# Expert matmuls in plain fp32 in four column quarters, and weight rows of 4 KB, in a two-layer decoder step

## What is computed

```python
logits = (t @ w_router).astype(jnp.float32)
top_logits, top_idx = lax.top_k(logits, TOP_K_EXPERTS)          # 2 of 8
gates = jax.nn.softmax(top_logits, axis=-1)
combine = jnp.sum(jax.nn.one_hot(top_idx, N_EXPERTS) * gates[..., None], axis=1)
for e in range(N_EXPERTS):
    out = out + combine[:, e:e + 1] * swiglu(t, w_gate[e], w_up[e], w_down[e])
# swiglu(h, g, u, d) = (silu(h @ g) * (h @ u)) @ d;  g, u: 1024 x 3584,  d: 3584 x 1024, all fp32
```

## Time and profile before

| | |
|---|---|
| time, median of 3 runs | 1491.48 us (1490.03 to 1492.24) |
| span of the profiled execution | 1489.5 us |
| experts, first matmul to the one before the last scatter | 532.7 to 1481.9 us of the span |
| weight tiles of the experts | 168 of 2 MB |

### The profile page before, as it was taken

The page is one execution under the profiler, slowest core; times in us unless marked ns, Lnnn a source line. Parts: engine busy times, 40 slices in busy tenths (PEclk is TensorE's granted clock), DMA queues, the critical chain, the costliest instruction groups (busy, mean ns, idle before and its releaser), DMA issues.

```text
span 1489.5 us, 21413 instructions
## 1 busy us (share of the span) xinstructions
PE 1476.5 (99%) x8116; PEld 1258.8 (85%) x8116; DVE 1196.2 (80%) x1088; ACT 975.1 (65%) x933; POOL 162.4 (11%) x159
## 2 busy tenths in 40 slices
PE   8999999999999999999999999999999999999998
PEld 6987699999988978888888888888888888888887
DVE  5698576665556688888888888888889888888987
ACT  5444464443455587777777777777777778777775
POOL 3653000000000048200001001001000000000100
PEclk9999999999999999999999999999999999999999
DMA  7562983427554379999999999999999999999990
GB/s 256 194 260 71 391 307 114 170 100 253 186 186 155 111 258 390 362 395 383 394 393 382 396 393 382 394 395 382 393 394 360 394 393 370 386 390 362 371 366 32
DMA packets 196822, 456.64 MB, mean 307 GB/s; under 512 B 9988, under 2 KB 13102, under 8 KB 196762
## 3 DMA queue, kind: packets, MB, share of 16 engines
q1 hardware_dynamic: 188912, 439.60, 79.6%
q0 software_dynamic: 4336, 13.15, 3.1%
q10 hardware_dynamic: 3514, 3.08, 0.7%
HBM read 443.78 MB, written 12.03 MB: 306 GB/s over the span
## 4 chain that ended last, share of the span: by engine, by line
PE 94%; DVE 2%; ACT 1%; SPq 1%; issue 1%; DMA 1%; DVEq 0%; ACTq 0%
PE bank L2041 25%; PE bank L2570 13%; PE bank L2572 13%; PE bank L2571 13%; PE bank L2584 7%; PE bank L2586 7%; PE bank L2585 7%; PE bank L2594 2%; PE bank L2246 1%; DMA ring<-in_attn_w_in 1%; PE bank L2258 1%; PE bank L2220 1%; PE bank L2339 0%; DVE wql L1827 0%; SPq L686 0%
## 5 line engine op out<-in xcount | busy, mean ns | idle before, releaser
L1827 DVE TENSOR_TENSOR wql<-ring,wqh 128x2048 fp32r<-128x2048 f32 x335 | 766.8, 2291 | 107.3 <-ACT wqh L994 106.5
L994 ACT ACTIVATE wqh<-ring 128x2048 fp32r<-128x2048 f32 x334 | 641.5, 1921 | 230.8 <-PE bank L2572 148.4
L2570 PE MATMUL bank<-wqh,xgh 128*128 128x512 f32 x892 | 353.7, 396 | 0.2 <-DVE wql L1827 0.2
L2571 PE MATMUL bank<-wql,xgh 128*128 128x512 f32 x896 | 349.2, 390 | 0.0
L2572 PE MATMUL bank<-wqh,xgl 128*128 128x512 f32 x892 | 348.0, 390 | 0.0
L2572 PEld LDWEIGHTS bank<-wqh,xgl 128*128 128x128 f32 x892 | 167.5, 188 | 35.9
L2570 PEld LDWEIGHTS bank<-wqh,xgh 128*128 128x128 f32 x892 | 167.5, 188 | 34.4 <-DVE wql L1827 1.0
L2571 PEld LDWEIGHTS bank<-wql,xgh 128*128 128x128 f32 x896 | 168.5, 188 | 32.9
L994 ACT ACTIVATE wd<-ring 128x1024 fp32r<-128x1024 f32 x90 | 95.1, 1059 | 133.4 <-PE bank L2041 133.4
L2584 PE MATMUL bank<-wqh,heTh 128*128 128x512 f32 x440 | 171.4, 389 | 0.0
L2586 PE MATMUL bank<-wqh,heTl 128*128 128x512 f32 x440 | 171.2, 389 | 0.0
(11 more groups left out here) (457 smaller groups left out, 1962.6 us busy)
## 6 DMA issues: line engine op xcount, KB each, us to landing
ring<-in_moe_w_gate SPq DMA_DIRECT2D x56, 2048.0 KB, 15.2
ring<-in_moe_w_up SPq DMA_DIRECT2D x56, 2048.0 KB, 15.1
ring<-in_moe_w_down SPq DMA_DIRECT2D x56, 2048.0 KB, 15.2
ring<-in_attn_w_in SPq DMA_DIRECT2D x6, 2048.0 KB, 15.8
ring<-in_ffn_w_gate SPq DMA_DIRECT2D x5, 2048.0 KB, 16.3
ring<-in_ffn_w_up SPq DMA_DIRECT2D x5, 2048.0 KB, 10.9
ring<-in_cache_k SPq DMA_DIRECT2D x16, 512.0 KB, 6.5
ring<-in_cache_v SPq DMA_DIRECT2D x16, 512.0 KB, 5.7
```

Source lines behind the costliest of these rows:

```text
L994: return nc.scalar.activation(dst, src, ACT.Copy)
L1827: return v.tensor_tensor(dst, src, head.bitcast(F32), ALU.subtract)
L2570: mm(bank, xgh[:, k, :], w_h[:, part], start=(k == 0), stop=False)
L2571: mm(bank, xgh[:, k, :], w_l[:, part], start=False, stop=False)
```

## The change

The items have 96 slots, as three groups of 32. Matmuls are plain fp32 on unsplit weights, read straight from the ring, and each uses one quarter of the array's columns: 32 slots stationary (128 x 32), 256 (or 128) weight columns streaming, the result in 32 partitions of a PSUM bank. A "round" of four such matmuls fills the four quarters. Quarters 0 to 2 hold the three slot groups on the same quarter of the chunk's weight columns; quarter 3 takes the one slot group that is left over for the fourth quarter of the columns, so that three rounds cover 3 groups x 4 column parts. Chunks are 1024, 1024, 1024 and 512 columns wide; the wide gate and up chunks come as two tiles of 512 rows x 4 KB (`h` is the half), the last one as a tile of 1024 rows x 2 KB as before. There are still 21 tiles of 2 MB per item. `head`, `tail`, `wqh`, `wql`, `q_head` and `q_tail` are gone; a ring buffer is free when PE has used the tile (`q_used`). Indirect DMAs move 96 rows instead of 128.

```diff
-NCH = DFE // CH
+WIDE = [1024, 1024, 1024, 512]
+FROM = [0, 1024, 2048, 3072]
+NCH = len(WIDE)
+ROUNDS = 3
...
+GRP = 32
+SL = 3 * GRP
+MAXBLK = (T + SL - 1) // SL
...
         def expert_tile(e, g, kind, c, h):
...
-                src = w[bass.ds(e, 1), :, CH * c:CH * c + CH].rearrange("o (k p) f -> p (o k) f", p=P)
-                sp.dma_start(tile_cols(s, CH), src).then_inc(got, 16)
+                k = SLOT // wide
+                src = w[bass.ds(e, 1), P * k * h:P * k * h + P * k, FROM[c]:FROM[c] + wide]
+                sp.dma_start(ring[s][:].rearrange("p (k f) -> p k f", k=k),
+                             src.rearrange("o (k p) f -> p (o k) f", p=P)).then_inc(got, 16)
...
-                sp.wait_ge(q_tail, i * HI + (U0 + 2 * (g - RING + 1)))
+                sp.wait_ge(q_used, i * PER_ITEM + (U0 + g - RING + 1))
...
-            pool.indirect_dma_start(out=z_rows, out_offset=bass.IndirectOffsetOnAxis(ap=slots_to[:, 0:1], axis=0),
-                                    in_=ysb[:], in_offset=None, compute_op=ALU.add).then_inc(z_in, 16)
+            pool.indirect_dma_start(out=z_rows, out_offset=bass.IndirectOffsetOnAxis(ap=slots_to[0:SL, 0:1], axis=0),
+                                    in_=ysb[0:SL, :], in_offset=None, compute_op=ALU.add).then_inc(z_in, 16)
...
         def silu(i, c):
-            nc.scalar.activation(he[:], banks[c % NCH % 2][:], ACT.Silu).then_inc(sg_ok, 1)
+            n = WIDE[c % NCH] // 4
+            act.wait_ge(*after(i, UP, c))
+            for r in range(ROUNDS):
+                nc.scalar.activation(he[:, r, 0:n], pair_banks(c)[r][:, 0:n], ACT.Silu).then_inc(sg_ok, 1)
...
-        def tail(i, n):
-
-            dve.wait_ge(q_head, i * HI + (n + 1))
-            minus(lo_buf(n), half_of(n // 2, n % 2), hi_buf(n)).then_inc(q_tail, 1)
...
-        def half_tile(i, n, kind, c, last_item=False):
...
+        def of_round(r, q):
+
+            return (q, r) if q < ROUNDS else (r, ROUNDS)
+
+        def gate_or_up(i, g, kind, c, h):
+
+            wide = WIDE[c % NCH]
+            n, ks = wide // 4, SLOT // wide
+            pe.wait_ge(*arrival(i, g))
+            w = ring[expert_slot(g)][:].rearrange("p (k f) -> p k f", k=ks)
+            for j in range(ks):
+                k = ks * h + j
+                for r in range(ROUNDS):
+                    out = pair_banks(c)[r][:, n * kind:n * kind + n]
+                    for q in range(4):
+                        tokens, cols_ = of_round(r, q)
+                        last = mm(out[GRP * q:GRP * q + GRP, :], xg[:, k, GRP * tokens:GRP * tokens + GRP],
+                                  w[:, j, n * cols_:n * cols_ + n], start=(kind == GATE and k == 0), stop=(k == KD - 1),
+                                  skip_group_check=True)
+            last.then_inc(q_used, 1)
+
+        def down(i, g, c, h, src, by_round=False):
...
+            for r, j in steps:
...
+                for q in range(4):
+                    tokens, cols_ = of_round(r, q)
+                    left = src[:, per * part + b, GRP * tokens:GRP * tokens + GRP] if part < ROUNDS else \
+                        src[:, per * tokens + b, SL:P]
+                    last = mm(sums_of(r)[GRP * q:GRP * q + GRP, :], left, w[:, j, 256 * cols_:256 * cols_ + 256],
+                              start=first, stop=(c == NCH - 1 and j == CH // P - 1), skip_group_check=True)
```

More of the change, by code:

```diff
@@ L621, in token_rows, with last_tile, after, pair_banks @@
         return htok[NS * low:NS * low + NS, 4, :]
[L623 to L642, removed]
+    def last_tile(kind, c):
+        return NPRO + max(n for n, tile in enumerate(BODY_TILES) if tile[:2] == (kind, c))
+    def after(i, kind, c):
+        return q_used, i * PER_ITEM + (U0 + last_tile(kind, c) + 1)
+    def pair_banks(c):
+        return banks[ROUNDS * (c % 2):ROUNDS * (c % 2) + ROUNDS]
+    def sums_of(r):
+        return banks[6 + r // 2][:, 256 * (r % 2):256 * (r % 2) + 256]
+    BASE = {q_used: U0, y_out: 2}
     def start_counters(engine, *sems):
@@ new lines, in scatter_samples @@
+            part, left = slice(CH * half, CH * half + CH), pickT[0:SL, NP + NS * (1 - half):NP + NS * (1 - half) + 2 * NS]
+            mm(bank[0:2 * NS, :], left, ysbh[0:SL, part], start=(half == 0), stop=False)
+            return mm(bank[0:2 * NS, :], left, ysbl[0:SL, part], start=False, stop=(half == 1))
+        def of_round(r, q):
[7 more added lines that the diff above has]
+                k = ks * h + j
+                for r in range(ROUNDS):
+                    out = pair_banks(c)[r][:, n * kind:n * kind + n]
[5 more added lines that the diff above has]
+            last.then_inc(q_used, 1)
@@ new lines, in down @@
+        def down(i, g, c, h, src, by_round=False):
+            per = WIDE[c] // 4 // P
+            pe.wait_ge(*arrival(i, g))
+            w = ring[expert_slot(g)][:].rearrange("p (k f) -> p k f", k=CH // P)
+            steps = [(r, j) for r in range(ROUNDS) for j in range(CH // P)] if by_round else \
+                [(r, j) for j in range(CH // P) for r in range(ROUNDS)]
+            for r, j in steps:
+                part, b = (CH // P * h + j) // per, (CH // P * h + j) % per
+                first = c == 0 and h == 0 and j == 0 and r != 1
+                for q in range(4):
[4 more added lines that the diff above has]
+                              start=first, stop=(c == NCH - 1 and j == CH // P - 1), skip_group_check=True)
+                if by_round and r == 1 and j == CH // P - 1:
+                    last.then_inc(y_half, 1)
@@ L2589, in half_tile @@
             last.then_inc(q_used, 1)
         def turn(i, c):
-            pe.wait_ge(he_ok, i * NCH + (c + 1))
-            for j in range(4):
-                last = tr(banks[6][:, P * j:P * j + P], he[:, P * j:P * j + P], ident[:])
+            per = WIDE[c] // 4 // P
+            for part in range(ROUNDS):
+                pe.wait_ge(he_ok, i * PARTS + (ROUNDS * c + part + 1))
+                for b in range(per):
+                    at, most = per * part + b, 2 * per
+                    last = tr(pair_banks(c)[at // most][:, P * (at % most):P * (at % most) + P], he[:, part, P * b:P * b + P], ident[:])
```

447 lines of the change are left out of this document (197 added, 250 removed).

## The result

| | before | with the change |
|---|---|---|
| time, median of 4 runs each | 1491.06 us (1490.03 to 1492.24) | 1559.22 us (1555.54 to 1562.45) |
| ratio | | 1.0457, 95% interval 1.0443 to 1.0471 |
| span of the profiled execution | 1489.5 us | 1553.4 us |
| first expert matmul to the last one | 532.7 to 1481.9: 949 us | 532.3 to 1545.9: 1014 us |

The kernel became 68 us slower; 79 us less had been forecast. The trunk and the tail are as long as before (532 us, and 7.5 against 7.6 us), so all of it lies in the experts. The page of the changed kernel: busy time, the slices of the granted clock and of GB/s, the queues, the chain, and the groups of matmuls of gate and up (L2550) and of down (L2569).

A forecast was written before the change was run, and what follows sets the result against it. PE bounds the kernel, DMA a close second; afterwards DMA: 535 + 822 (tiles) + 19 (POOL's transfers) + 22 (boundaries) = 1398, plus 1 + 2.6 + 8.5 = 1410, plus 2 = 1412 us; range 1392 to 1450.

The forecast's parts named there:

- PE, matmuls: Expert matmuls on PE: 0.216 us per round of four, 2.6 us per tile instead of 5.45, 57.6 us per item.
- upper bound of 113.0 us per item: PE's expert work if each of 1104 matmuls per item cost 0.0995 us, plus 3.2 us; the lower bound was taken instead.
- starts of rounds of four 0.216 us apart at length: Sign in PE's expert timeline that the forecast holds; 0.43 would say the clock rival, uneven starts the PE-feeding rival.
- 402 matmuls at 0.0995: Earlier trace's 40 us of mixed and larger PE shapes, 0.0995 us each, used as evidence against PE being unfed.
- Rival C: Expert stage: PE cannot be fed, slower than today above 0.1046 us per matmul; 1522 us at 0.108; chance 0.06.
- DVE, ACT: cost 0: Experts: subtractions and copies go, small steps come; nothing gained directly, transposes' waits for `he` stay covered, cost 0.
- Ring: cost 0: Weight ring: buffers held until PE has used them, yet six tiles still queued at the DMA engines, cost 0.
- DMA: Expert weight loads: 5.07 us per 4 KB-row tile, 5.43 per 2 KB-row tile, 107.2 us per item plus 3.2 for scatter and gather.
- Rival A: Gate and up loads: strided 4 KB rows no better than 2 KB rows, 32 us more, 1444 us; chance 0.12.
- A boundary: Between expert items: scatter and gather disturb the weight stream by 3.2 us, seven times, 22 us.
- Rival B, the clock: Expert stage: half-busy PE drops to half clock, 115.3 us per item; 1466 us if held through; chance 0.06.
- Tail: After the last expert matmul: 7.6 us today plus about 0.9 for moving 32 x 256 pieces, 8.5 us.

The follow-up runs named there:

- e6: e2 with the narrow chunk's inner gate and up blocks as half as many 256-column matmuls, same column count: 1449.38 us, ratio 0.9725.
- e1: The changed kernel with expert matmuls reading the upper halves of the fp32 operands as bf16, one record per matmul: 1437.81 us, ratio 0.9647.
- e7: The kernel before, with PE's loop holding two items per turn and the last two items written out: 1499.4 us, ratio 1.0063.
- e2: The changed kernel with PE's loop over the items written out eight times, so no jump: 1493.6 us, ratio 1.0008.
- e5: The changed kernel with its jump, but after the first 25 expert tiles each load brings only 64 columns: 1484.82 us in one run.
- e3: The changed kernel with rounds 1 and 2 left out except for each sum's first and last block, all DMAs kept: 1438.72 us, ratio 0.9657.
- e4: e3 with the wide gate and up chunks loaded as 2 KB rows instead of 4 KB: 1464.27 us, ratio 0.9826.
- e8: e3 with the accumulating scatter after each of the first seven items replaced by a plain 4 KB store: 1428.07 us, ratio 0.9576.

## Why the prediction was wrong

Two steps failed. The first puts PE level with DMA and is worth 11 us of the result; the second is worth 110.

**The first is "PE, matmuls"**: "16 of them take 1.07 us". The rows are right, the noun is not. The earlier trace rows say x16, and the program's loop over the heads makes 8 matmuls of that shape per batch: each plain fp32 matmul leaves two records. I took records for matmuls, and so read 0.216 us per round where it is 0.432. Both numbers lay open, the records in the trace and the loop in the code, and I divided only one by the other's unit. The 512-column rows that seemed to confirm it share the mistake (x32 for 16 matmuls). The fp32r matmuls before leave one record each, so nothing in their rows gives a warning. With 112.0 in place of 57.6 us per item PE would have come out level with DMA (my 110.4), and the sum at 532.7 + 896 + 8.5 + 2 = 1439 us or more, a gain of 3.5% at best. e6 is this case, with PE fed: 1449.4 us, still inside my 1392 to 1450. e1 shows the step from the other side: one record per matmul, and the forecast picture appears. The Trainium skill says the same in its own way: its page "FP8 and Floating Point Precision", section "TensorE Precision Notes", has true fp32 take four passes through the array. Estimated from that page, a round of 256 columns is 1024 cycles, 0.43 us at 2.4 GHz, and the trace agrees with 0.432 us. I had not weighed that rule, and it spoke against this change. That my upper bound of 113.0 us per item comes so near to the 112.0 is luck: it was worked out from 402 records of other shapes, which I took for matmuls as well. And one sign that I had set, "starts of rounds of four 0.216 us apart at length", is there to the letter, since it was made with the same mistake.

**The second is that the sum has nothing for feeding PE**, on the ground of "402 matmuls at 0.0995". Rival C had it as "PE cannot be fed" from 0.1046 us per matmul on, chance 0.06, and its outcome came about: (1014/8 - 3.2)/1104 = 0.112 us, of which 252 x 0.432/1104 = 0.099 are the fp32 work itself. Its reasons were not the right ones. All four quarters overlap and issuing is no limit by itself (e1); the code of an item no longer stays with the engine and is fetched anew, 16 KB at a time, at every turn (e7), slowly after a jump (e2 minus 66 us) and too slowly for 128-column matmuls (e6 minus 44 us more), all the slower as weights fill the DMA engines (e5). The 402 of the earlier trace rows were no argument: those 40 us took three instruction packets, one per 13 us, and an item of the changed kernel takes 19 in 130 us, one per 7 us. The Trainium skill, page "Runtime: NRT & Kernel Launch", section "Instruction fetch mechanics", tells of blocks of 16 KiB, 128 KiB for PE, and says that a jump to a place outside the current two pages stops the engine until the page has come. The runs agree on the packet and on the stop. They don't agree on the two pages: the kernel before jumps back over 79 KB, five packets, and fetches nothing, so the border lies between 79 and 158 KB. Nor do they agree that fetching is otherwise mostly hidden, as the section has it: e2 has no jump and stands 30 us.

**DVE, ACT: cost 0** was right: DVE is at 27%, ACT at 21% of the span, and PE has no wait for the three parts of `he`.

**Ring: cost 0** was right where it can be seen, in e3 and e1, where a tile lands 24.3 us after its start, so the queue stays deep. In the changed kernel PE gives the buffers back late, and only some two tiles are queued (10.0 us to landing).

**DMA: right in kind, 24 us too low.** The last tile's matmuls would start at 1399 and start at 1422.5 us in e3. Tiles of 4 KB rows take 5.13 and not 5.07 us, 9 us in all; the instruction packets, not in the sum, are 3 us there (1.16 MB); some 12 us are not traced to a cause. The saving by 4 KB rows was put at 89 x 0.36 = 32 us and is 25.6 us (e4 against e3), 0.29 us per tile. Rival A is refuted. The rule of the Trainium skill that was weighed in the prediction (page "DMA: Bandwidth & Descriptors", section "Why small descriptors are slow (HBM only)") had 2.2% for it; the runs do not agree, they say 5.3% (0.29 of 5.42). A boundary was put at 3.2 us; its scatter costs 1.5 (e8), its gather was not tried.

**Rival B, the clock**, happened: the granted clock falls when PE waits, to 0.82 over the span in e1 and 0.90 in e3. It cost nothing there, since DMA sets the pace in both, and the two differ by 1 us. In the changed kernel, where PE is on the path, it cost 23 us after the waits. **Tail**: 7.5 us instead of 8.5.

In short, of the 147 us between forecast and result, 27 are DMA's floor (e3), 11 are PE's work in fp32 that lies above it (e6), and 110 are instructions that come late (44 in the narrow chunk, 66 by the jump), with the half clock behind these waits in them. The parts are differences between runs, and in another order of the runs they would be somewhat different.

## What to carry to other kernels

Count the records of an operation against the program's loop before a duration is taken from them: a plain fp32 matmul is two, and its cost per column twice what one record shows. Count PE's instructions per loop turn too, since a change that halves the time of a matmul but doubles their number can outgrow what the engine holds; then it waits at each jump and wherever its matmuls are short, all the more beside a full DMA stream. If it must be many small matmuls, write the loop out, and give the narrow parts wider columns.

## What the runs showed of the hardware that was not expected

- Instruction code is traffic: 185 packets of 16 KB, against 39 before. With a full weight stream the two waits after a jump are 4.95 + 3.02 us, with a nearly idle one 2.16 + 1.66 us.
- Four 32-column quarters do work side by side at length: 96 records of 0.379 us pass in 5.36 us, over a whole tile as in the short bursts.
- One short wait can cost the full clock: in e7 PE was busy all through, waited 2.91 us, and the matmuls behind that wait start 0.43 us apart instead of 0.227. Behind the wait of 0.90 us at the second jump the clock stayed full.
- With PE about half busy (47% in e1) the granted clock was 0.74, and the time was still DMA's.
